# A decoder layer on one Trainium2 core: ScalarE's copy of the even attention tile's transposed weights is put ahead of the scan's decays

## The reference

```python
h = rmsnorm(x)
p = h @ w_in            # q latent | kv latent | rope key | z | x,B,C | dt | gates
A = latent_attention(...)   # 16 heads, causal, 4 query blocks of 128 tokens
B = ssm_branch(...)         # conv on x/B/C, then a chunked scan:
#   per chunk of 128 tokens, per head:
    cs    = cumsum(dt * a)
    decay = exp(where(tri, cs[l] - cs[s], -inf))
    y     = (C B^T * decay) @ xdt  +  C exp(cs) @ state
    state = state * exp(cs[-1]) + B^T (exp(cs[-1] - cs) * xdt)
mix = (sigmoid(ga) * (A @ w_a) + sigmoid(gb) * (B @ w_b)) @ w_out
x = x + rmsnorm(mix);  x = x + rmsnorm(relu(rmsnorm(x) @ w_up)**2 @ w_down)
```

## Time and profile before

| | |
|---|---|
| median of 3 runs | 1441.14 us (1437.75 to 1443.85) |
| the profiled execution | 1438.54 us, its span 1436.8 us |
| TensorE busy | 1375.8 us (96%) |
| VectorE busy | 856.9 us (60%) |
| ScalarE busy | 572.8 us (40%) |
| GpSimd busy | 615.9 us (43%) |

### The profile page before, as it was taken

One profiled execution on the slowest core, in us unless ns is written; L12 is line 12 of the kernel. 1 busy time (PEld: TensorE's weight loads), 2 busy tenths in 40 slices (PEclk: granted clock), 3 DMA queues, 4 the chain that ended last, 5 costly groups with the idle time before them and its releaser, 6 DMA issues. The chain is left out here.

```text
span 1436.8 us, 28643 instructions
## 1 busy us (share of the span) xinstructions
PE 1375.8 (96%) x11458; PEld 1283.9 (89%) x11458; DVE 856.9 (60%) x1744; ACT 572.8 (40%) x1186; POOL 615.9 (43%) x753
## 2 busy tenths in 40 slices
PE   7997999999999999999999999999899999999996
PEld 7996898988889889898989877999899999999995
DVE  6877887888888887888885443233522222222226
ACT  5454454635555445454645222223323322232231
POOL 6551353543525344353543222445134445444562
PEclk9999999999999999999999999999789999999998
DMA  4333232332333234232345899343113222332231
GB/s 164 106 99 99 80 120 75 109 121 81 108 100 121 80 94 135 80 121 77 107 138 160 268 354 347 118 143 94 45 59 102 87 92 89 99 93 89 89 103 60
DMA packets 113812, 168.92 MB, mean 118 GB/s; under 512 B 17648, under 2 KB 86768, under 8 KB 113680
## 3 DMA queue, kind: packets, MB, share of 16 engines
q1 hardware_dynamic: 56016, 127.32, 27.8%
q10 hardware_dynamic: 57664, 39.78, 9.3%
HBM read 154.26 MB, written 12.81 MB: 116 GB/s over the span
## 5 line engine op out<-in xcount | busy, mean ns | idle before, releaser
L497 POOL TENSOR_TENSOR w_lo<-w_stage,w_hi 128x256 fp32r<-128x256 f32 x728 | 594.0, 848 | 790.4 <-ACT w_hi L1085 788.5
L560 PE MATMUL lin<-act_hi,w_hi 128*128 128x260 f32 x1664 | 348.4, 291 | 9.9 <-DVE arena L1713 4.4
L560 PE MATMUL lin<-act_lo,w_hi 128*128 128x260 f32 x1664 | 338.7, 286 | 0.0
L560 PEld LDWEIGHTS lin<-act_hi,w_hi 128*128 128x128 f32 x1664 | 261.1, 192 | 20.1 <-issue 17.1
L1085 ACT ACTIVATE w_hi<-w_stage 128x1024 fp32r<-128x1024 f32 x180 | 189.5, 1053 | 191.3 <-PE lin L560 120.1
L560 PEld LDWEIGHTS lin<-act_lo,w_hi 128*128 128x128 f32 x1664 | 261.7, 192 | 0.0
L560 PE MATMUL lin<-act_hi,w_lo 128*128 128x260 f32 x1664 | 221.8, 286 | 0.0
L560 PE MATMUL lin<-mid_hi,w_hi 128*128 128x260 f32 x1024 | 208.5, 285 | 1.1 <-issue 1.1
L560 PEld LDWEIGHTS lin<-act_hi,w_lo 128*128 128x128 f32 x1664 | 208.9, 190 | 0.0
L560 PE MATMUL lin<-mid_lo,w_hi 128*128 128x260 f32 x1024 | 205.6, 282 | 0.0
L560 PEld LDWEIGHTS lin<-mid_hi,w_hi 128*128 128x128 f32 x1024 | 157.9, 188 | 2.9 <-issue 2.3
(11 more groups left out here) (317 smaller groups left out, 1933.6 us busy)
## 6 DMA issues: line engine op xcount, KB each, us to landing
w_stage<-in_wall SPq DMA_DIRECT2D x184, 512.0 KB, 3.6
arena<-in_cache ACTq DMA_DIRECT2D x80, 144.0 KB, 4.3
arena<-in_state ACTq DMA_DIRECT2D x16, 512.0 KB, 5.2
out_stateT<-arena ACTq DMA_DIRECT2D x16, 512.0 KB, 4.4
o_attn<-in_cache SPq DMA_DIRECT2D x64, 128.0 KB, 4.2
arena<-in_cache SPq DMA_DIRECT2D x64, 128.0 KB, 4.0
arena<-in_cache SPq DMA_DIRECT2D x48, 144.0 KB, 4.1
arena<-in_xT SPq DMA_DIRECT2D x8, 520.0 KB, 6.0
```

Source lines behind the costliest of these rows:

```text
L497: low = pool.tensor_tensor(w_lo[:, slot, part], w_stage[:, slot, part], w_hi[:, slot, part].bitcast(F32), ALU.subtract)
L560: mm = pe.matmul(lin[:, pl.slot, hf, 0:HALF], w[:, ch.slot, off:off + P], r[:, hf * HALF:(hf + 1) * HALF], start=(k == 0 and p == 0), stop ...
```

## The change

`weights_out(u)` of the even tile is called behind `exponent(u + 1)` and ahead of the wait for `a_seg`, `ecs` and the decays, in place of behind them. In chunks 0 to 2 it had been called from `raw_evac`, in chunk 3 directly; both calls go. Nothing else is changed on any engine.

```diff
                     if i == 1 and c == 0:
                         for t in range(2):
                             samples_in(t, 0)
+                    weights_out(u)
                     act.wait_ge(S["a_seg"], g * 4 + (c + 1))
                     act.activation(ecs[:, :, :], lin[:, pl.slot, 0, :].rearrange("p (h l) -> p h l", h=HPG),
                                    ACT.Exp).then_inc(S["a_ecs"], 1)
...
                     decay.then_inc(S["a_exp"], 1)
                     if c < NCH - 1:
-                        raw_evac(c + 1, between=lambda: weights_out(u))
+                        raw_evac(c + 1)
                     else:
-                        weights_out(u)
                         round_chunk(c_chunk(i, "z1" if has_in else "ga5"))
                     output_out(u)
```

## The result

The changed kernel took 1463.85 us as the median of 4 runs (1462.82 to 1465.56); the kernel before, run beside it, took 1442.49 (1437.75 to 1443.87). The ratio is 1.016, with a 95% interval of 1.0137 to 1.0183. The direction was forecast. The size was not: 9.3 us were expected and 21.4 came. The profiled execution of the changed kernel took 1465.56 us with a span of 1463.8, 27.0 us longer than the 1436.8 of before. That is 5.6 us more than the medians differ by: the profiled execution of before lies 4.0 us under its median, the changed kernel's 1.7 us over.

What follows compares the result with a forecast made beforehand. The prediction took TensorE, busy 96% of the span, as the bound. Group costs of 6.65 + 0.85 + 0.77 + 1.05 = 9.32 us on the median of 1441.14 gave 1450.5 us, range 1442 to 1455.5.

Steps and rivals of the forecast that it cites:

- (1): Sign in the changed profile: TensorE's wait for the weight copy (L1306) goes from 13.3 us to nearly nothing.
- (2): Sign: ScalarE waits for TensorE's transposes 20 us or more, 1.9 in each chunk 0, 0.5 to 1 in most chunks 1.
- (3): Sign: TensorE gets waits at scan_back for Mt (L1872), about 0.5 us in chunk 0 and 1.0 in chunk 2.
- (4): Sign: TensorE's wait at L744 for L1850 in chunk 2, 0.25 us in i = 4, grows to 1.0 to 1.4 us.
- (5): Sign: a group is 0.8 to 1.5 us longer.
- TensorE's slack to the squares: At the group statistics behind chunk 3: 0.53 us of slack to ScalarE's squares, so the statistics start 1.33 us later.
- Weight loading does not bind: Weight roundings on ScalarE come 1.4 to 1.7 us later, but the projection needing them starts several us after them.
- this group's 1.05 us: Cost for i = 8, without convolution or samples behind it: the middle of 0.77 and 1.33 us.
- the chain: Lateness passed from ScalarE's waiting copy through Mt and VectorE to TensorE: 1.33 us in most groups, 9.32 us in all.
- The gain: Rival: the copy stops being late and nothing takes its place, 13.3 us off, 1427.8 us; chance 0.08.
- Local cost only: Rival: VectorE makes up its lag, each chunk pays only for its own Mt, 2.8 us in all, 1443.9; chance 0.21.
- Larger: Rival: VectorE ends each group 1.79 us late and TensorE keeps no slack, 14.3 us in all, 1455.4; chance 0.1.

Runs made afterwards that it cites:

- e9: Kernel before with the early copy in chunks 2 and 3 of groups 1 to 7 only, last convolution tap behind scan_back(3): 1441.02 us, ratio 0.9998.
- e12: Kernel before with row_max(u + 2) earlier, last tap behind scan_back(3), and copy early in chunk 2 of groups 1 to 7: 1431.48 us, ratio 0.9942.
- e4: Kernel before, copy in its old place, with ScalarE making each of the two squares ahead of the group statistics twice: 1458.9 us, ratio 1.0124.
- e5: Changed kernel with VectorE's last convolution tap in chunk 3 moved behind scan_back(3): 1456.99 us, ratio 1.0112 to the kernel before.
- e3: Kernel before with the early copy in chunks 2 and 3 alone: 1454.92 us, ratio 1.0101.
- e10: Changed kernel with the old order in the last group (i = 8) alone: 1457.87 us, ratio 1.0132 to the kernel before.
- e1: Kernel before with the early copy in chunk 0 alone: 1448.69 us, ratio 1.006.
- e2: Kernel before with the early copy in chunk 1 alone: 1446.29 us, ratio 1.0038.
- e7: Kernel before with the early copy in chunks 2 and 3 alone and the last convolution tap behind scan_back(3): 1448.51 us, ratio 1.0052.
- e6: Kernel before with only VectorE's last convolution tap in chunk 3 moved behind scan_back(3): 1440.54 us, ratio 0.9996.
- e11: Kernel before with VectorE's row_max(u + 2) earlier in chunks 1 and 2 and the last tap behind scan_back(3): 1430.54 us, ratio 0.9926.

## Why the prediction was wrong

**What held.** The reading of the chunks did, nearly to the row. In i = 4, against the shift of the group's start (8.24 us), scan_back(0) came +0.51 later (+0.5 forecast), chunk 1's transposes +0.50, chunk 2's +1.41 (+1.42), scan_back(2) +1.43 (+1.59), scan_back(3) +0.94 (+1.09). Of the five signs, (1) came: 13.3 us to none. (2) came: ScalarE waits 23.6 us for transposes, 1.85 in chunk 0 and 0.52 in chunk 1 of i = 4. (3) came: waits for `Mt` of 0.43 and 0.95. (4) came: 0.25 became 1.10. e9 and e12 show the core of the argument by itself: the wait for the copy and the wait for `Mt` stand one behind the other, so taking the first away moves TensorE by one step only. (5), a group 0.8 to 1.5 us longer, failed: between statistics the groups are 1.9 to 3.9 us longer.

**The step that failed: nothing was charged for TensorE's clock.** The prediction saw that TensorE's slack to the squares would be used up, and counted the wait behind it at its own length. That wait stands ahead of two microseconds of one-column products, and behind it the clock fell in five of seven groups. In the profile the clock accounts for 13.7 of 27.0 us, 10.2 of them behind the statistics. e4 makes the same loss without the copy, and e5 takes it out of the changed kernel and keeps VectorE's lateness in the chunks. Over all traces it is the same: in the four kernels with a wait ahead of the statistics (after, e3, e4, e10) the clock fell behind 19 of these 28 waits (i = 1 to 7), and in the ten kernels without one it fell behind none of 70 statistics. Why it fell behind 19 and not all 28 stays open.

**A term that was mis-sized: the squares.** Statistics in i = 4 came +1.74 later, not +1.33. `Mt` was +1.64, but the squares +2.13 (444.28 against 433.91 in the earlier trace rows, less 8.24). The 0.5 us between lie in the convolution. VectorE and GpSimd, first before and then after, with the squares last:

```profile
428.19 0.55 DVE L1746 TENSOR_SCALAR arena<-arena,small 128x544 f32<-128x544 f32 x1
...
428.61 4.25 POOL L497 TENSOR_TENSOR w_lo<-w_stage,w_hi 128x256 fp32r<-128x256 f32 x4 [9.49 <-ACT w_hi L1085]
```

```profile
438.07 1.07 DVE L1746 TENSOR_SCALAR arena<-arena,small 128x544 f32<-128x544 f32 x1
...
438.12 3.96 POOL L497 TENSOR_TENSOR w_lo<-w_stage,w_hi 128x256 fp32r<-128x256 f32 x4 [9.50 <-ACT w_hi L1085]
...
444.28 1.25 ACT L1358 ACTIVATE arena<-arena 128x520 f32<-128x520 f32 x2 [2.96 <-DVE arena L1890]
```

The same operation takes 1.07 us in place of 0.55 when GpSimd's split of the weights runs beside it. It is so throughout: from 150 to 800 us of both traces the 21 operations of this line that run beside GpSimd nearly from end to end take 1.03 to 1.08 us, and the 33 that touch its work for 0.13 us at most take 0.55 or 0.56. Before, one in each group is slow; after, the one in chunk 3 is too. No run took GpSimd's work away, so this rests on the rows. The whole stretch from the even transposes of chunk 0 to the statistics grew by 12.6 us over the eight groups, where the sum had 9.3; 1.7 of the 12.6 are the fall of the clock in i = 1.

**"Weight loading does not bind" was wrong in i = 8,** and this group's 1.05 us with it. I had checked the slack of the projection that uses the weights, and not what is queued on ScalarE behind their rounding. The roundings came late, then the load into the freed stage, then `mid_hi`, then VectorE's root. e10 puts it at 6.0 us (4.1 if each kernel is taken against its own runs of before), and e9 at 7.5 in the other setting.

**The sum.** Take 6.0 us for i = 8 and 10.2 for the clock behind the statistics off the 1463.85, and 1447.7 are left, beside a forecast of 1450.5. In the profiles, 27.0 less 10.2 for that clock, 1.7 for the clock in i = 1 and 6.4 for i = 8 (its chunks and all behind them) leaves 8.7, where the forecast had 8.3 for i = 1 to 7. So the chain was sized about right and two things were left out of it; that it comes so close is partly luck, since single executions differ by more. The range ended at 1455.5 since its upper bound was still a sum of chain lengths, 1.79 us a group.

**The rivals.** The gain fell to e1, e2 and e3 together: no part of the change is faster. *Local cost only* fell to the waits at L744, which doubled from 5.5 to 11.1 us. *Larger* comes nearest in size, but 8.5 us short of the time: i = 4 reached the statistics +1.74 late, close to that rival's 1.79, and the rest was not VectorE's lag.

## What to carry to other kernels

Moving a step ahead on an in-order engine also moves a wait ahead: list all that is queued behind it, down to the last reader of each result, before calling any of it hidden. When two waits stand one behind the other, taking the first away pays only as far as the second is earlier, so look for the engine whose chain feeds both; here a reordering on VectorE gave 0.7% where the one on ScalarE lost 1.6%. Where the slack ahead of thin matmuls runs out, price the clock too; a wait that can't be avoided cost no clock here when it stood between dense passes.

## What the runs showed of the hardware

- A wait of 0.62 to 0.72 us, directly ahead of 2.0 us of one-column products, brought the granted clock to 0.50 behind it in 19 of 28 cases (five of seven after, four in e3, five in e4 and in e10). From statistics to L816 that was about 1.5 us each time (7.58 against 6.03), once 3.1 us (9.11, in i = 6). Without a wait there, none of 70 such stretches had a fall. A wait of 0.85 us between dense passes, at L816 in i = 1 to 7 of e5, e7 and e9, brought no fall behind any of 21; e5's granted clock was 1.00 from 180 to 790 us.
- The clock also fell where TensorE had waited for 0.3 us at most: behind 24 products of 128 columns and 6 of 16 (L703), which come some 14 us behind the statistics. That was 14 times in nine of the fourteen traces (e1, e2, e4, e6 to e9, e11 and e12), 1.7 us each. So one profile's count of falls is not the kernel's: e6, as fast as before, had three in the scan (one of them in i = 1, behind a wait of 3.0 us as before has it), and the profiled execution of before had none.
- VectorE's small operations slow down beside GpSimd's subtractions. In e7's root, operations on 65x8 take 0.66 us while GpSimd is at work (until 785.96), 0.16 just after, and 0.65 when it is at work again (from 786.89):

```profile
785.33 0.66 DVE L1546 TENSOR_TENSOR st<-st 65x8 f32<-65x8 f32 x1
786.02 0.16 DVE L1547 SCALAR_TENSOR_TENSOR st<-st 65x8 f32<-65x8 f32 x1
...
787.66 0.65 DVE L1547 SCALAR_TENSOR_TENSOR st<-st 65x8 f32<-65x8 f32 x1
```

```profile
782.70 3.26 POOL L497 TENSOR_TENSOR w_lo<-w_stage,w_hi 128x256 fp32r<-128x256 f32 x4 [4.79 <-ACT w_hi L1085]
786.89 2.76 POOL L497 TENSOR_TENSOR w_lo<-w_stage,w_hi 128x256 fp32r<-128x256 f32 x4 [0.93 <-ACT w_hi L1085]
```

The Trainium skill, "SBUF — State Buffer", in its section "SBUF: two separate sides", describes ports that VectorE and GpSimd share, held by one of them for a whole instruction while the other waits; of VectorE's operations it says so for those with two inputs in SBUF and for certain fast modes. The rows agree as far as they go: an operation of 0.16 us takes up to 0.5 us longer, which is less than one of the four subtractions (0.8 us each, 3.26 / 4). So a chain of twelve such operations and `diag` grows wherever it slides under GpSimd's work. From its first operation to the end of `diag`, the root of i = 8 took 3.07 us before (780.17 to 783.24), 5.40 after and 6.30 in e7, which is part of the wait at L816.
